# A 31-tap depthwise convolution on TensorE in 16 passes of two taps instead of 31 of one, with its passes and VectorE's taps at other places in the attention, and the first weight slab used chunk by chunk

## The chip, the cores and the metric

The kernel runs on one core of a Trainium2 chip. The metric is the device time in microseconds (us) of one execution. The engines are TensorE (PE in the profile; its weight loads are PEld), VectorE (DVE), ScalarE (ACT), GpSimd (POOL) and SyncE (SP, which issues most DMAs). Each takes its own instructions in order and waits for others by semaphores.

## The reference

Two transformer blocks over 512 positions of width 1024 run one after the other, all in float32. The first has a 3-tap convolution branch, a stick-breaking attention and an MLP; the second a parallel mixer, a cross attention over 256 memory rows and a gated MLP. The mixer of the second block is where most of the change lies:

```
z = h @ w_in                                  # h: 512 x 1024, RMS-normed
a = z[:, :512] * sigmoid(z[:, 512:1024])      # 512 channels
a[t, c] = sum_k conv_dw[k, c] * a[t + k - 15, c] + b[c]     # k = 0 .. 30
a = silu(layernorm(a))                        # over the 512 channels
q, k = rope(rmsnorm(q)), rope(rmsnorm(k))     # 8 query heads, 2 key/value heads of 64
att = softmax(q @ k.T / 8) @ v                # no mask, 512 x 512 scores per head
y = concat(a, att) @ w_out
```

The other part of the change lies at the first product of the first block, `h @ w_in`, with h the normed and modulated input.

## The kernel before

**Products.** A float32 product is made of three fp32r matmuls (`mm3`, L811 to L814): high by high, high by low and low by high parts. POOL splits each 1 MB weight slab of 128 x 2048 into `w_hi` (L687, for slab 0 L695) and `w_lo` (L689, for slab 0 L700), in the order in which PE uses them; three slabs are in flight. ACT and DVE split the activations into `ht_hi` and `ht_lo`, eight chunks of 128 x 512.

**First slab.** Slab 0 holds four chunks of 128 rows (k = 0 to 3) of four output groups (m = 0 to 3) of `h @ w_in`. POOL makes its low part in four pieces, one for each m, and counts them in `first_lo`. In `features` (called with `first=True`), PE takes group 0 with its four chunks, each as soon as its chunk of h is split, then groups 1, 2 and 3. So each group has its own bank of PSUM (PE's output memory, eight banks) and is finished with slab 1.

**The 31-tap convolution.** Channels lie on the partitions in four chunks, positions along the row, padded by 15 on both sides (`av`). POOL does chunk 3. DVE does chunks 0 and 1, 62 taps, each one scalar-tensor-tensor instruction of 128 x 512 (L1857) that adds into bank 7. PE does chunk 2: a pass of plain float32 for each tap, with a diagonal 128 x 128 matrix as weights (`tap_of`, made by ACT from the identity in L1651) and the shifted 512 columns of `av` as moving data, all into bank 6 (L1234). A plain float32 matmul leaves two MATMUL records in the trace.

**Attention of the second block.** Four pairs of heads; a pair has four score tiles (n = 0 to 15 over all pairs), one for each 128 queries, and each tile has two halves, one for each head (32 halves in all). `ATT2_ORDER` (L225 to L235) sets the order for every engine:

- `zz` n: PE makes the scores of tile n, two matmuls of 64 rows (L1195). For each half DVE takes the maximum (TENSOR_REDUCE, L2223), scales it (L1864) and, one half later, inverts the sum of the half before (RECIPROCAL, L1868). ACT does the exponential (L1697). The probabilities are scaled by ACT for pairs 0 and 1 and by POOL for pairs 2 and 3.
- `conv` n: PE does `PE_TAPS[n]` taps (3, 3, 3, 3 with pair 0; 3, 3, 2, 2 with pair 1; 2, 1, 1, 1 with pair 2; 2, 1, 1 with pair 3). After the last, ACT adds the bias and stores the chunk.
- `tt` n: PE transposes the probabilities of the pair before (L1209), ACT copies them out (L1715). `oo` p: PE multiplies pair p with the values, four key chunks by two heads of 64 columns (L1221). ACT and DVE split the result.
- `l` 0: PE sums the convolution's output over the channels (L1248). It waits until all four chunks are complete. `l` 1 sums the squares.

The scores of pair p + 1 stand between the transposes of pair p, and `oo` p - 1 stands behind the first score tile of pair p + 1. Of DVE's 62 taps, 20 stand between the rotary steps and 16 behind the keys. The other 26 are spread by `fill(per_tile)`, where `per_tile` works out to 1: one tap behind each half, which is used up with half 26. What is left of them is done before DVE's part of `l` 0 (`for _ in taps`).

Of the kernel before, what the change touches and what calls it, by code (L numbers as in the profile page):

```python
# [19 lines left out]
ALU = mybir.AluOpType  # L20
# [5 lines left out]
P = 128  # L26
# [240 lines left out]
def build(nc, A, out):  # L267
    with ExitStack() as ctx:
# [126 lines left out]
        with ExitStack() as lend:  # L395
# [270 lines left out]
        def _(g):  # L666
# [128 lines left out]
        def _(pe):  # L795
# [27 lines left out]
            def features(t0, ks, ah, al, i=None, tper=0, sper=0, n=T, each=None, first=False, behind=None):  # L823


                for s in range(ks):
# [546 lines left out]
        def _(act):  # L1373
# [243 lines left out]
            act.wait_ge(tables_loaded, 16 * 6)  # L1617
            st.done(act.activation(rope_gq[:], rope[:, 0], ACT.Copy, scale=qkg[:, 0:1]), tables_made)
# [105 lines left out]
            for what, n in ATT2_ORDER:  # L1724
# [120 lines left out]
        def _(v):  # L1845
# [603 lines left out]
```

## Time and profile before

| | |
|---|---|
| runs | 1513.2, 1512.0, 1512.74 us, median 1512.74 |
| the profiled execution | 1516.2 us, its span 1514.5 us |
| PE busy | 1463.9 us, 97% of the span |
| POOL, DVE, ACT busy | 917.3, 736.0, 452.0 us |
| PE's share of the chain that ended last | 85% (DVE 8%, ACT 3%, DMA 2%) |
| the second block's attention, from its first scores to `l` 0 | 879.8 to 949.0 us |

The span is one profiled execution; its own time lies 1.7 us above its span and 3.5 us above the median of the three timed runs. PE is busy nearly everywhere. So a stretch in which PE waits for another engine, or in which the chain of waits runs over another engine, is an exception and is to be read by itself: there the share over the whole span says nothing.

### The profile page before, as it was taken

Reading aid. Unit: us, or ns where it says so; the run is one execution under the profiler, and the core shown is the slowest. Engines: PE = TensorE matmul, PEld = TensorE weight load, DVE = VectorE, ACT = ScalarE, POOL = GpSimd, SP = SyncE. Lnnn points to the kernel's source line nnn. Section 1 sums busy time; section 2 is a strip of 40 time slices with the busy share of each in tenths; the row PEclk is TensorE's granted clock in tenths of the full one; section 3 lists DMA queues with packets and bytes.
Section 4 is the critical chain, followed back from the end, with each engine's and each line's share of the span. In section 5 each row is a group of like instructions: output and inputs, shape, how many; then the busy total and the mean of one; then the engine's idle time right before and its main releaser. Section 6 shows DMA issues by size and latency. Waiting matters only on the chain.

```text
span 1514.5 us, 18342 instructions
## 1 busy us (share of the span) xinstructions
PE 1463.9 (97%) x7071; PEld 1187.7 (78%) x7071; DVE 736.0 (49%) x1121; ACT 452.0 (30%) x924; POOL 917.3 (61%) x361
## 2 busy tenths in 40 slices
PE   3999999999999999999999999999999999999997
PEld 3788777768898888888898854689779888888886
DVE  6898146544541211212262877532416555455656
ACT  3201133323520110201142466533324433333213
POOL 1857454345656565656566997266234889788651
PEclk9999999999999999999999999999999999999999
DMA  9765221223322323232243200123023423232131
GB/s 332 299 252 219 98 84 56 84 84 99 125 98 84 111 84 112 84 111 84 84 147 112 84 29 1 56 94 130 28 84 112 139 84 112 84 111 84 56 102 65
DMA packets 94099, 162.59 MB, mean 107 GB/s; under 512 B 3597, under 2 KB 44481, under 8 KB 94017
## 3 DMA queue, kind: packets, MB, share of 16 engines
q1 hardware_dynamic: 90896, 155.20, 30.1%
q10 hardware_dynamic: 3121, 6.26, 1.2%
q8 instruction: 56, 0.92, 0.2%
q14 instruction: 26, 0.21, 0.0%
HBM read 159.35 MB, written 2.10 MB: 107 GB/s over the span
## 4 chain that ended last, share of the span: by engine, by line
PE 85%; DVE 8%; ACT 3%; DMA 2%; issue 1%; POOL 0%; DVEq 0%; SPq 0%; ACTq 0%; POOLq 0%
PE bank L812 26%; PE bank L813 26%; PE bank L814 26%; DVE bank L1857 2%; DMA ada_w<-in_w_ada 1%; DVE smx L2223 1%; PE bank L1221 1%; DVE x L1853 1%; DVE bank L1853 1%; PE bank L1291 1%; PE bank L1272 1%; PE bank L1065 1%; PE bank L1088 1%; ACT junk L1402 1%; PE bank L1248 0%
## 5 line engine op out<-in xcount | busy, mean ns | idle before, releaser
L689 POOL TENSOR_TENSOR w_lo<-w_raw,w_hi 128x2048 fp32r<-128x2048 f32 x111 | 516.8, 4656 | 9.3
L687 POOL TENSOR_SCALAR w_hi<-w_raw 128x2048 fp32r<-128x2048 f32 x111 | 216.0, 1946 | 480.4 <-DMA w_raw<-in_w_in 116.5
L812 PE MATMUL bank<-ht_hi,w_hi 128*128 128x512 f32 (+1 forms) x1200 | 444.1, 370 | 0.8 <-DVE ht_lo L1853 0.8
L813 PE MATMUL bank<-ht_hi,w_lo 128*128 128x512 f32 (+1 forms) x1200 | 441.0, 368 | 0.0
L814 PE MATMUL bank<-ht_lo,w_hi 128*128 128x512 f32 (+1 forms) x1200 | 440.8, 367 | 0.0
L812 PEld LDWEIGHTS bank<-ht_hi,w_hi 128*128 128x128 f32 x1200 | 227.1, 189 | 42.7 <-DVE ht_lo L1853 2.6
L814 PEld LDWEIGHTS bank<-ht_lo,w_hi 128*128 128x128 f32 x1200 | 227.0, 189 | 37.2
L813 PEld LDWEIGHTS bank<-ht_hi,w_lo 128*128 128x128 f32 x1200 | 227.2, 189 | 36.8 <-issue 0.5
L1857 DVE SCALAR_TENSOR_TENSOR uc<-bank,par,uc 128x511 f32<-128x511 f32 x88 | 66.0, 750 | 128.1 <-ACT uc L1801 125.4
L1853 DVE TENSOR_TENSOR facc<-bank,facc 128x512 f32<-128x512 f32 x64 | 44.3, 692 | 114.9 <-PE bank L814 111.2
L814 PE MATMUL bank<-w_lo,hq_hi 128*128 128x512 f32 x256 | 99.6, 389 | 0.0
L812 PE MATMUL bank<-w_hi,hq_hi 128*128 128x512 f32 x256 | 99.6, 389 | 0.0
L813 PE MATMUL bank<-w_hi,hq_lo 128*128 128x512 f32 x256 | 99.6, 389 | 0.0
L1594 ACT ACTIVATE hr<-bank 128x512 f32<-128x512 f32 x32 | 19.2, 599 | 261.8 <-PE bank L814 261.0
L812 PE MATMUL bank<-w_hi,ht_hi 128*128 128x512 f32 x224 | 88.2, 394 | 0.0
L1801 ACT ACTIVATE uc<-bank,par 128x512 f32<-128x512 f32 x44 | 34.4, 781 | 177.3 <-PE bank L814 177.1
L814 PE MATMUL bank<-w_lo,ht_hi 128*128 128x512 f32 x224 | 87.2, 389 | 0.0
L813 PE MATMUL bank<-w_hi,ht_lo 128*128 128x512 f32 x224 | 87.2, 389 | 0.0
L1857 DVE SCALAR_TENSOR_TENSOR ada_acc<-ada_w,cvec,ada_acc 128x1024 f32<-128x1024 f32 x42 | 80.3, 1911 | 11.5 <-DMA ada_w<-in_w_ada 8.2
L1853 DVE TENSOR_TENSOR bank<-bank,hr 128x512 f32<-128x512 f32 x32 | 22.4, 700 | 122.4 <-ACT hr L1594 122.3
L757 POOL TENSOR_TENSOR dn_lo<-dn_raw,dn_hi_all 128x1024 fp32r<-128x1024 f32 x28 | 67.0, 2406 | 18.0 <-ACT dn_hi_all L1780 17.9
L1853 DVE TENSOR_TENSOR ht_lo<-bank,ht_hi 128x512 fp32r<-128x512 f32 x60 | 41.5, 692 | 32.3 <-ACT ht_hi L1540 20.3
(294 smaller groups left out, 2216.0 us busy)
## 6 DMA issues: line engine op xcount, KB each, us to landing
w_raw<-in_w_in SPq DMA_DIRECT2D x27, 1024.0 KB, 5.0
ada_w<-in_w_ada SPq DMA_DIRECT2D x48, 512.0 KB, 7.2
w_raw<-in_w_up SPq DMA_DIRECT2D x22, 1024.0 KB, 4.9
w_raw<-in_w_mlp_in SPq DMA_DIRECT2D x16, 1024.0 KB, 5.4
w_raw<-in_w_mlp_out SPq DMA_DIRECT2D x16, 1024.0 KB, 5.0
w_raw<-in_w_out SPq DMA_DIRECT2D x8, 1024.0 KB, 5.0
w_raw<-in_w_mem_kv SPq DMA_DIRECT2D x8, 1024.0 KB, 5.1
dn_raw<-in_w_down SPq DMA_DIRECT2D x16, 512.0 KB, 4.8
```

The costliest lines, as they stand in the source:

```text
L687: g.tensor_scalar(w_hi[:, r], w_raw[:, r], 1.0, 1.0, ALU.mult, ALU.mult).then_inc(slab_hi, 1)
L689: g.tensor_tensor(w_lo[:, r], w_raw[:, r], w_hi[:, r].bitcast(F32), ALU.subtract).then_inc(slab_split, 1)
L757: g.tensor_tensor(dn_lo[:, w], dn_raw[:, w], dn_hi(w).bitcast(F32), ALU.subtract).then_inc(dn_split, 1)
L812: inc_free(pe.matmul(o, ah, bh, start=start, stop=False))
L813: pe.matmul(o, al, bh, start=False, stop=False)
L814: return pe.matmul(o, ah, bl, start=False, stop=stop)
L1065: pe.matmul(t.ap[:, 0:W1[qt]], q1[o, p, qt * P:qt * P + P], k1[o, p, 0:W1[qt]], start=True, stop=True).then_inc(t.full, 1)
L1088: ins = pe.matmul(t.ap[HD * j:HD * j + HD, kc * P:T], v1[:, kc, h * HD:h * HD + HD], at1[:, j, A1[kc]:A1[kc + 1]], start=kc == 0, stop=kc ...
L1594: st.done(act.activation(hr[:, m % 2], t.ap[:], ACT.Relu), hr_ready)
L1801: st.done(act.activation(uc[:, c], tiles[c].ap[:], ACT.Identity, scale=par[:, p, 2 + g, k:k + 1], bias=par[:, p, 6 + g, k:k + 1]), uc_ready)
L1853: do(v.tensor_tensor(o, a, b, op), sem, tile)
L1857: do(v.scalar_tensor_tensor(out=o, in0=a, scalar=s, in1=b, op0=op0, op1=op1), sem, tile)
```

## The change

**First slab.** POOL makes the low part in four pieces by chunk k (all four groups) instead of by group m. PE takes a chunk's products for the groups begun so far as soon as this chunk is there: first (0, 0), then (0, 1), (1, 0), (1, 1), and so on, as (m, k).

**Convolution on PE.** `av2` holds chunk 2 twice: partitions 0 to 63 have the channels of one half g, partitions 64 to 127 the same channels shifted by one position. Four DMAs on ACT's queue copy it. The weights are 128 x 64: two diagonals, one for tap 2k and one for tap 2k + 1. One pass for g = 0 writes partitions 0 to 63 of bank 6, one for g = 1 partitions 64 to 127. So there are 16 pairs of passes, 32 matmuls of 64 output rows. ACT makes 32 weight matrices of 128 x 64 instead of 31 of 128 x 128, and some small operands for them (`ident2`, `tap_w`, two DMAs to `cdw_x`).

**Places.** PE's pairs stand behind the tiles 0 to 8, as 3, 3, 3, 2 with pair 0, 1, 1, 1, 1 with pair 1 and 1 with tile 8. DVE's 26 late taps: none with pair 0, one behind each half of pairs 1, 2 and 3 (24), and the last two before `l` 0.

```diff
-PE_TAPS = (3, 3, 3, 3, 3, 3, 2, 2, 2, 1, 1, 1, 2, 1, 1)
+TAP_PAIRS = (K2 + 1) // 2
+PE_TAP_PAIRS = (3, 3, 3, 2, 1, 1, 1, 1, 1)
...
-                for m in range(4):
-                    c = slice(m * P, m * P + P)
-                    g.tensor_tensor(lo[:, :, c], raw[:, :, c], hi[:, :, c].bitcast(F32), ALU.subtract).then_inc(
-                        first_lo if m < 3 else slab_split, 1)
+                for k in range(4):
+                    g.tensor_tensor(lo[:, k], raw[:, k], hi[:, k].bitcast(F32), ALU.subtract).then_inc(
+                        first_lo if k < 3 else slab_split, 1)
...
+                    if by_pieces:
+                        for new in range(4):
+                            each(new)
+                            Tile(t0 + new).wait_free(pe)
+                            pe.wait_ge(first_lo if new < 3 else slab_split, new + 1 if new < 3 else 1)
+                            for m, k in [(m, new) for m in range(new)] + [(new, k) for k in range(new + 1)]:
+                                c = slice(m * P, m * P + P)
+                                mm3(Tile(t0 + m).ap[:, 0:n], wh[:, k, c], wl[:, k, c], ah[:, k], al[:, k], k == 0, False)
...
-                    pe.wait_ge(taps_made, K2)
-                    Tile(T0["w_in2a"] + 4 + DVE_CC).wait_taken(pe)
-                k0 = sum(PE_TAPS[:i])
-                for k in range(k0, k0 + PE_TAPS[i]):
-                    ins = pe.matmul(t.ap[:], tap_of(k), av[:, DVE_CC, k:k + T], start=k == 0, stop=k == K2 - 1)
-                if k == K2 - 1:
+                    pe.wait_ge(taps_made, 2 * TAP_PAIRS)
+                    pe.wait_ge(av2_loaded, 16 * 4)
+                k0 = sum(PE_TAP_PAIRS[:i])
+                for k in range(k0, k0 + PE_TAP_PAIRS[i]):
+                    for g in range(2):
+                        ins = pe.matmul(t.ap[HC * g:HC * g + HC, :], tap_m[:, k, g], av2[:, g, 2 * k:2 * k + T], start=k == 0,
+                                        stop=k == TAP_PAIRS - 1)
+                if k == TAP_PAIRS - 1:
...
-            for k in range(K2):
-                w = V_CDW + CC * k + DVE_CC
-                st.done(act.activation(tap_of(k), ident[:], ACT.Copy, scale=vec[:, w:w + 1]), taps_made)
+            Tile(T0["w_in2a"] + 4 + DVE_CC).wait_taken(act)
+            avc = av[:].rearrange("p c t -> p (c t)")
+            for half in range(2):
+                for g in range(2):
+                    at = DVE_CC * (T + 2 * pad) + half
+                    act.dma_start(av2[HC * half:HC * half + HC, g, :],
+                                  avc[HC * g:HC * g + HC, at:at + T + 2 * pad]).then_inc(av2_loaded, 16)
...
+            for k in range(TAP_PAIRS):
+                for g in range(2):
+                    st.done(act.activation(tap_m[:, k, g], ident2[:], ACT.Copy, scale=tap_w[:, k, g:g + 1]), taps_made)
...
-            per_tile = -(-(DVE_CC * K2 - sum(TAPS_BEFORE_ROPE) - TAPS_BEHIND_K) // (H1 * NT))
...
-                        fill(per_tile)
+                        fill(n >= NT)
```

Line numbers of the changed file differ: L812 is L811, L1195 is L1202, L1234 is L1242, L1209 is L1216, L1857 is L1886, L2223 is L2251.

On PE, at the second and third group of three matmuls of slab 0 (bank 2 is group m = 0, bank 3 is group 1), before:

```order
L812 MATMUL bank2<-ht_hi,w_hi 128x512
L813 MATMUL bank2<-ht_hi,w_lo 128x512
L814 MATMUL bank2<-ht_lo,w_hi 128x512
L812 MATMUL bank2<-ht_hi,w_hi 128x512
L813 MATMUL bank2<-ht_hi,w_lo 128x512
L814 MATMUL bank2<-ht_lo,w_hi 128x512
```

and now:

```order
L811 MATMUL bank2<-ht_hi,w_hi 128x512
L812 MATMUL bank2<-ht_hi,w_lo 128x512
L813 MATMUL bank2<-ht_lo,w_hi 128x512
L811 MATMUL bank3<-ht_hi,w_hi 128x512
L812 MATMUL bank3<-ht_hi,w_lo 128x512
L813 MATMUL bank3<-ht_lo,w_hi 128x512
```

The second group is the same, (0, 1); the third was (0, 2), which needs chunk 2 of h, and is (1, 0), which needs chunk 0.

On PE, at the first score tiles of pair 0 (bank 6 is the convolution's, `x3` counts like instructions in a row), before:

```order
L1195 MATMUL bank4<-k2,q2 128x512
L1195 MATMUL bank5<-k2,q2 128x512
L1234 MATMUL bank6<-av,tap_low 128x512 x3
L1195 MATMUL bank0<-k2,q2 128x512
L1195 MATMUL bank1<-k2,q2 128x512
L1234 MATMUL bank6<-av,tap_low 128x512
L1234 MATMUL bank6<-av,not_before 128x512
L1234 MATMUL bank6<-av,tap_m 128x512
```

and now:

```order
L1202 MATMUL bank4<-k2,q2 128x512
L1202 MATMUL bank5<-k2,q2 128x512
L1242 MATMUL bank6<-av2,tap_m 64x512 x6
L1202 MATMUL bank0<-k2,q2 128x512
L1202 MATMUL bank1<-k2,q2 128x512
L1242 MATMUL bank6<-av2,tap_m 64x512 x6
```

Three taps of 128 output rows behind a tile became six matmuls of 64 output rows, which do six taps.

On DVE, at the last three halves of pair 3 and DVE's part of `l` 0 (`ay<-bank2,ay`), before:

```order
L2223 TENSOR_REDUCE smx<-bank1 128x1
L1864 TENSOR_SCALAR smx<-smx,qks 128x1
L1868 RECIPROCAL smx<-smx 128x1
L2223 TENSOR_REDUCE smx<-bank4 128x1
L1864 TENSOR_SCALAR smx<-smx,qks 128x1
L1868 RECIPROCAL smx<-smx 128x1
L2223 TENSOR_REDUCE smx<-bank5 128x1
L1864 TENSOR_SCALAR smx<-smx,qks 128x1
L1868 RECIPROCAL smx<-smx 128x1 x2
L1857 SCALAR_TENSOR_TENSOR ay<-bank2,ay 128x512 x4
```

and now:

```order
L2251 TENSOR_REDUCE smx<-bank4 128x1
L1893 TENSOR_SCALAR smx<-smx,qks 128x1
L1897 RECIPROCAL smx<-smx 128x1
L1886 SCALAR_TENSOR_TENSOR bank7<-av,vec,bank7 128x512
L2251 TENSOR_REDUCE smx<-bank5 128x1
L1893 TENSOR_SCALAR smx<-smx,qks 128x1
L1897 RECIPROCAL smx<-smx 128x1
L1886 SCALAR_TENSOR_TENSOR bank7<-av,vec,bank7 128x512
L1897 RECIPROCAL smx<-smx 128x1
L1886 SCALAR_TENSOR_TENSOR bank7<-av,vec,bank7 128x512
L1886 SCALAR_TENSOR_TENSOR ay<-av,vec,bank7 128x512
L1886 SCALAR_TENSOR_TENSOR ay<-bank2,ay 128x512 x4
```

Behind each half stands a tap (`bank7<-av,vec,bank7`), and two more stand between the last reciprocal and `l` 0; before, no tap stood here.

## Rows read from the trace of the kernel before

**Rows 1.** which lines hold the chain of waits, 880 to 970 us, by share

```profile
by line: DVE smx L2223 18.7%; DVE bank L1857 17.0%; PE bank L1221 16.2%; PE bank L1248 8.1%; ACT pt L1715 7.1%; DVE smx L1864 6.0%; issue 5.6%; PE bank L1195 4.7%; DVE smx L1868 3.9%; PE bank L1209 3.2%; ACT p2d L1697 1.9%; PE bank L1234 1.
```

**Rows 2.** busy time in one stretch: us, PE, PEld, DVE, ACT, POOL, PEclk, DMA

```profile
931.70:949.00 17.30, 15.79 (x72) 7.35 (x72) 12.60 (x31) 11.51 (x26) 5.77 (x9) 1.00 0.01 1
```

**Rows 3.** timeline of PE, 879 to 950 us: start, us, engine, line, tiles, idle before

```profile
879.82 1.13 PE L1195 MATMUL bank<-k,q 64*128 64x512 f32 x4
...
880.88 2.84 PE L1234 MATMUL bank<-av,tap_low 128*128 128x512 f32 x6
...
883.65 1.13 PE L1195 MATMUL bank<-k,q 64*128 64x512 f32 x4
...
916.77 3.65 PE L1221 MATMUL bank<-pt,v 128*64 128x512 f32 x16 [1.40 <-ACT pt L1715]
...
922.43 1.12 PE L1234 MATMUL bank<-av,tap_m 128*128 128x512 f32 x2
...
949.04 3.70 PE L1248 MATMUL bank<-ay,ones 128*128 128x512 f32 x8 [0.31 <-ACT pt L1715]
```

**Rows 4.** timeline of DVE, 868 to 952 us

```profile
868.35 1.55 DVE L1857 SCALAR_TENSOR_TENSOR bank<-av,vec,bank 128x512 f32<-128x512 f32 x2
...
880.98 0.69 DVE L2223 TENSOR_REDUCE smx<-bank 128x1 f32<-128x512 f32 x1 [3.39 <-PE bank L1195]
...
898.15 0.69 DVE L2223 TENSOR_REDUCE smx<-bank 128x1 f32<-128x512 f32 x1
...
914.97 0.69 DVE L2223 TENSOR_REDUCE smx<-bank 128x1 f32<-128x512 f32 x1
...
921.08 0.69 DVE L1853 TENSOR_TENSOR ht_lo<-bank,ht_hi 128x512 fp32r<-128x512 f32 x1 [2.28 <-ACT ht_hi L1540]
...
922.53 0.69 DVE L2223 TENSOR_REDUCE smx<-bank 128x1 f32<-128x512 f32 x1 [0.76 <-PE bank L1195]
...
935.40 0.69 DVE L2223 TENSOR_REDUCE smx<-bank 128x1 f32<-128x512 f32 x1
...
941.76 0.69 DVE L2223 TENSOR_REDUCE smx<-bank 128x1 f32<-128x512 f32 x1 [0.77 <-PE bank L1195]
...
947.74 0.69 DVE L2223 TENSOR_REDUCE smx<-bank 128x1 f32<-128x512 f32 x1 [0.41 <-PE bank L1195]
...
951.04 0.17 DVE L1868 RECIPROCAL smx<-smx 128x1 f32<-128x1 f32 x1 [0.60 <-ACT p2d L1697]
```

**Rows 5.** timeline of ACT at the diagonal matrices, 838 to 852 us

```profile
839.54 7.72 ACT L1651 ACTIVATE tap_m<-ident,vec 128x128 f32<-128x128 f32 x26
...
851.88 0.59 ACT L1496 COPY k<-bank 128x512 f32<-128x512 f32 x1 [4.62 <-PE bank L1153]
```

**Rows 6.** timeline of ACT's queue near 44 us, one DMA issue

```profile
44.13 0.35 ACTq L1392 DMA_DIRECT2D ada_b<-in_b_ada  x1
```

**Rows 7.** timeline of PE in the first slab, 42 to 47 us

```profile
42.42 0.79 PE L812 MATMUL bank<-ht_hi,w_hi 128*128 128x512 f32 x1 [0.49 <-DVE ht_lo L1853]
...
45.14 0.63 PE L812 MATMUL bank<-ht_hi,w_hi 128*128 128x512 f32 x1
45.57 0.63 PE L813 MATMUL bank<-ht_hi,w_lo 128*128 128x512 f32 x1
...
46.54 0.40 PE L813 MATMUL bank<-ht_hi,w_lo 128*128 128x512 f32 x1
46.77 0.40 PE L814 MATMUL bank<-ht_lo,w_hi 128*128 128x512 f32 x1
```

**Rows 8.** timeline of POOL in the first slab

```profile
36.69 4.97 POOL L700 TENSOR_TENSOR w_lo<-w_raw,w_hi 128x512 fp32r<-128x512 f32 x4
```

**Rows 9.** line L1221 on PE's weight port: count, ns min/median/max

```profile
L1221 PEld LDWEIGHTS bank<-pt,v x64: 132/137/137, 916.7 to 963.8; 128*64 128x64 f32 x64
```

**Rows 10.** busy time in two stretches near 230 us, columns as in group 2

```profile
228.00:232.00 4.00, 1.34 (x8) 0.89 (x7) 3.83 (x4) 1.09 (x2) 1.98 (x1) 1.00 0.00 0
232.00:236.00 4.00, 3.34 (x22) 3.04 (x24) 1.90 (x3) 2.34 (x8) 0.00 (x0) 0.74 0.00 0
```

More of the change, by code:

```diff
@@ L41 @@
 DVE_CC = CC - POOL_CC - PE_CC
-PE_TAPS = (3, 3, 3, 3, 3, 3, 2, 2, 2, 1, 1, 1, 2, 1, 1)
+TAP_PAIRS = (K2 + 1) // 2
+PE_TAP_PAIRS = (3, 3, 3, 2, 1, 1, 1, 1, 1)
 POOL_PAIRS = 2
-LOW_TAPS = 4
 ADA_BUFS = 7
@@ L229 @@
             ATT2_ORDER += [("zz", NT * (_p + 1) + _m)]
-            ATT2_ORDER += [("conv", NT * (_p + 1) + _m)] * (NT * (_p + 1) + _m < len(PE_TAPS))
+            ATT2_ORDER += [("conv", NT * (_p + 1) + _m)] * (NT * (_p + 1) + _m < len(PE_TAP_PAIRS))
         ATT2_ORDER += [("oo", _p - 1)] * (_m == 0 and _p >= 1)
@@ L325, in build @@
         with ExitStack() as lend:
-            tap_low = sb("tap_low", [P, LOW_TAPS, P], where=lend)
-        with ExitStack() as lend:
             s2 = sb("s2", [P, 2, 2 * P], where=lend)
@@ L406, in build @@
         pt2 = sb("pt2", [P, 2, NT, T], where=ph)
-        tap_m = sb("tap_m", [P, K2 - LOW_TAPS - 1, P], where=ph)
+        HC = P // 2
+        tap_m = sb("tap_m", [P, TAP_PAIRS, 2, HC], where=ph)
+        av2 = sb("av2", [P, 2, T + 2 * pad], where=ph)
+        tap_w = sb("tap_w", [P, TAP_PAIRS, 2], where=ph)
+        cdw_x = sb("cdw_x", [P, K2 * CC], where=ph)
+        ident2 = sb("ident2", [P, HC], where=ph)
         ph.close()
@@ L447, in build @@
             "gated", "y_gated", "o_hi", "a1_sig", "a1_scanned", "sm_max", "sm_inv", "sm_p"))
-        taps_made = sem("taps_made")
+        taps_made, av2_loaded = sem("taps_made"), sem("av2_loaded")
         tables_made, q_squared, rope_std, ln_std = (sem(n) for n in (
@@ L518, in sums_made @@
             return sum(0 if not by_sums(r) else 2 if r % 2 == 0 else 4 for r in range(j))
-        def tap_of(k):
-            return tap_low[:, k] if k < LOW_TAPS else not_before[:] if k == LOW_TAPS else tap_m[:, k - LOW_TAPS - 1]
         block = ctx.enter_context(nc.Block())
@@ L834, in features @@
                     wh, wl = wv(r, 4)
+                    if by_pieces:
[6 more added lines that the diff above has]
+                                mm3(Tile(t0 + m).ap[:, 0:n], wh[:, k, c], wl[:, k, c], ah[:, k], al[:, k], k == 0, False)
+                        state["owed"] += 1
+                        continue
                     for m in range(4):
@@ L838, in features @@
                             t.wait_free(pe)
-                        if by_pieces:
-                            pe.wait_ge(first_lo if m < 3 else slab_split, m + 1 if m < 3 else 1)
                         for k in range(4):
@@ L1609, in _ @@
                                   A[name].rearrange("(p o) -> p o", o=1)).then_inc(tables_loaded, 16)
+            for g in range(2):
+                act.dma_start(cdw_x[HC * g:HC * g + HC, :],
+                              vec[HC - HC * g:P - HC * g, V_CDW:V_CDW + K2 * CC]).then_inc(tables_loaded, 16)
             t0 = T0["w_in2a"]
@@ L1616, in _ @@
                 st.done(act.activation(t.ap[:], t.ap[:], ACT.Sigmoid), gated)
-            act.wait_ge(tables_loaded, 16 * 6)
+            act.wait_ge(tables_loaded, 16 * 8)
             st.done(act.activation(rope_gq[:], rope[:, 0], ACT.Copy, scale=qkg[:, 0:1]), tables_made)
@@ L1648, in _ @@
             st.done(act.activation(t.ap[:], t.ap[:], ACT.Sqrt, bias=eps_t[:, 0:1], scale=1.0 / HD), rope_std)
-            for k in range(K2):
-                w = V_CDW + CC * k + DVE_CC
-                st.done(act.activation(tap_of(k), ident[:], ACT.Copy, scale=vec[:, w:w + 1]), taps_made)
+            Tile(T0["w_in2a"] + 4 + DVE_CC).wait_taken(act)
[5 more added lines that the diff above has]
+                                  avc[HC * g:HC * g + HC, at:at + T + 2 * pad]).then_inc(av2_loaded, 16)
+            own = vec[:, V_CDW:V_CDW + K2 * CC].rearrange("p (k c) -> p k c", c=CC)
+            other = cdw_x[:].rearrange("p (k c) -> p k c", c=CC)
+            st.done(act.activation(tap_w[:, TAP_PAIRS - 1, :], ident[:, 0:2], ACT.Copy, scale=0.0))
+            st.after()
+            for half in range(2):
+                h = slice(HC * half, HC * half + HC)
+                st.done(act.copy(ident2[h, :], ident[h, h]))
+                for g in range(2):
+                    st.done(act.copy(tap_w[h, 0:TAP_PAIRS - half, g], (own if g == half else other)[h, half::2, DVE_CC]))
+            st.after()
+            for k in range(TAP_PAIRS):
+                for g in range(2):
+                    st.done(act.activation(tap_m[:, k, g], ident2[:], ACT.Copy, scale=tap_w[:, k, g:g + 1]), taps_made)
             for g in range(KV2):
@@ L1735, in _ @@
                 elif what == "conv":
-                    if n == len(PE_TAPS) - 1:
+                    if n == len(PE_TAP_PAIRS) - 1:
                         t = Tile(T0["conv31_pe"])
```

## The prediction

> **What bounds the kernel now.** I read the busy table first: PE is busy for 97% of the span, so most edits that take PE work away would pay in full. The exception is the place where this change works. The chain of waits through the second block's attention, 880 to 970 us, has DVE's maxima (L2223) with 18.7% and DVE's taps (L1857) with 17.0% ahead of any line of PE; PE's convolution (L1234) is the last one named, with under 2% [rows 1]. So DVE sets the pace here, though PE looks busy beside it. The timeline of DVE says where. From the first half of pair 1 at 898.15 to the first half of pair 2 at 914.97 eight halves pass in 16.82 us, 2.10 us each, with no wait [rows 4]: maximum, scale, reciprocal and one tap. In pair 3, where the taps have run out, the four halves from 941.76 to 947.74 take 5.98 us, 1.50 us each, and the wait printed there is one for PE's scores (0.41) [rows 4]: from there on PE sets the pace, with 15.79 us busy of 17.30 against DVE's 12.60 [rows 2]. So pairs 0 to 2 are DVE's, pair 3 is PE's, and `l` 0 follows at once on PE at 949.04, 0.31 us late [rows 3].
>
> **The change part by part.** I call DVE's unit a half (32 of them) and PE's unit a tile (16).
>
> *PE's passes.* Three taps behind tile 0 take 883.65 - 880.88 = 2.77 us, the score pair 880.88 - 879.82 = 1.06, together 3.83 a tile. Two records, one tap, show 1.12 us and six show 2.84, so a tap more costs 0.86 [rows 3]. Nothing in the program before has the new form exactly, but L1221 has its shape: 128 rows by 64 columns, alternately into the lower and upper half of one bank, plain float32. Its 16 records, 8 matmuls, take 3.65 us [rows 3], 0.91 for two of them, where 0.86 each would be 6.9. So the two halves run side by side, and a pair of passes costs one tap of before. Blocks of 3 pairs stay at 2.77, the block of 2 is 2.77 - 0.86 = 1.9. Fifteen taps' worth of PE time, 15 x 0.86 = 13 us, are gone, mostly behind tiles 4 to 14.
>
> *Pair 0.* Tile 3's scores start at 879.82 + 3 x 3.83 = 891.3. DVE follows 1.16 us behind (880.98 against 879.82), 892.5, and with no tap between its last two halves it needs from the first maximum of a tile to the end of the pair's last reciprocal what it needed in pair 3: 951.04 + 0.17 - 947.74 = 3.47 us [rows 4]. Pair 1 starts on DVE at 896.0 instead of 898.15: gain 2.1 us. The end of tile 4's scores, 891.3 + 1.06 + 1.9 + 1.06 = 895.3, is not later. The eight taps taken out of pair 0 gain no more than that, since PE's three-pair blocks fill the room.
>
> *Pairs 1 and 2.* A tap stands behind each half before and after; DVE keeps 2.10 us a half, and PE's shorter blocks only make PE wait. The stalls at `oo` 0 (2.28 and 0.76 us [rows 4]) hang on ACT's copies behind DVE's last reciprocal of the pair, so they move with DVE. Nothing gained, nothing lost: pair 3 starts at 935.40 - 2.1 = 933.3.
>
> *Pair 3.* Its first two halves had taps already, so half 27 starts at 941.76 - 2.1 = 939.66. Then six halves now carry a tap: 6 x 2.10 = 12.6, to 952.3. The last reciprocal adds 0.2, and the two taps left over 1.55 + 0.1 (868.35 shows two in a row in 1.55 [rows 4]): 954.2. PE may not start `l` 0 until the last of them is done. So `l` 0 starts at 954.2 instead of 949.04, **5.2 us later**. Behind `l` 0 stands everything: the value product of pair 2, the transposes of pair 3, the layer norm and w_out. PE waits for no transfer there that could take this back. Bounds: 4.5 if DVE comes out of pair 0 another 0.7 earlier (the reciprocal hidden), 6.0 if the new blocks cost 0.3 more per tile for switching shapes.
>
> *First slab.* PE waited 0.49 us at 42.42 for chunk 2 of h [rows 7]; now it has (1, 0) and (1, 1) to do meanwhile. In the stretch it runs at 45.57 - 45.14 = 0.43 us a matmul and later at 46.77 - 46.54 = 0.23 [rows 7], 1.2 and then 2.4 GHz. If the faster clock comes at the same moment, 0.49 us of slow work is worth 0.49 x 0.23 / 0.43 = 0.26 us; if it comes earlier by the whole wait, 0.5; if it comes 2 us earlier since PE works without a break, another 2 x (1 - 0.23 / 0.43) = 0.9, 1.4 in all. I take 0.5, the wait itself, nearest to the row. POOL's pieces are the same size, 4.97 / 4 = 1.24 us each, the last at 41.7 [rows 8], before PE needs it.
>
> *ACT's new work.* 32 weight matrices at 7.72 / 26 = 0.30 us each against 31, seven small copies at no more than 0.30, four DMA issues at 0.35 [rows 6] and about 0.3 of waiting: 0.3 + 2.1 + 1.4 + 0.3 = 4.1 us. ACT sat idle for 4.62 us before its next work at 851.88 [rows 5]. I cost it at nothing; if that cover is short by 0.5 us, the keys' copies are late by as much, and PE has its w_in slabs to do. At the other end it is nothing too. The copies to `av2` have from about 840 to 880.9 to land. Storing PE's chunk moves from tile 14 to tile 8 and stands where ACT waits for `oo` 0 anyway.
>
> Sum: -2.1 (pair 0) + 7.3 (pair 3 and the two leftover taps: 954.2 + 2.1 - 949.04) - 0.5 (slab 0) = **+4.7 us**. For the profiled execution 1516.2 + 4.7 = 1520.9; it lay 3.5 above the median of the runs, so the median becomes 1512.74 + 4.7 = 1517.4.
>
> One rule speaks against the side-by-side passes. In L1221 the 64 weight loads last 0.137 us each [rows 9], and all of them fit beside the matmuls within those 3.65 us a product. The Trainium skill (TensorE: Matmul & The Clock Gate, Part 3, What overlaps and what doesn't) says that a weight load overlaps running matmuls only where it goes to another row group. Both column halves use all rows; by that rule 12 loads of a three-pair block would stand open, 12 x 0.137 = 1.6 us a tile. Row and rule differ here; I follow the row and keep the rule as a small rival.
>
> **The rivals.**
>
> *A, forecast:* as above, 1517.4, its own range 1515.8 to 1519.2.
>
> *B, the clock falls in pair 3.* PE's work there is 1.9 of 4.2 us a tile: 5.98 / 2 = 2.99 before, less a one-tap block of 2.77 - 2 x 0.86 = 1.05. For it: near 230 us PE was busy 1.34 of 4 us and the next 4 us were granted 0.74 [rows 10]. Against: with waits of 1.4 us the stage kept 1.00, as [rows 2] shows for pair 3. At half speed the pair itself stays hidden behind DVE, but `l` 0 (3.6 us) could take twice as long: 1517.4 + 3.6 = 1521.0.
>
> *C, the stalls between pairs close.* If shorter PE blocks let `oo` 0 and `oo` 1 come earlier, DVE's 2.28 + 0.76 and 0.77 us [rows 4] go: -3.8, that is 1513.6, no measurable change. Against: those waits end with ACT's copies, behind DVE's own last reciprocal.
>
> *D, faster: PE sets the pace in pair 3 also after the change.* Price: l 0 comes 2.1 us earlier from pair 0, and two one-tap blocks of 1.05 us (tiles 13 and 14) are gone, -4.2, with slab 0 -4.7: 1508.0. It needs the tap to fit into DVE's wait for scores. It decides at 1.50 us a half in pair 3: below that with a tap, the kernel is faster; at 2.10, A holds. Only 0.41 us a tile of waiting is there for two taps.
>
> *E, the change does not do what it says: the passes of a pair run one after the other.* A block of 3 pairs is 6 x 0.86 = 5.2, a tile 6.3, the block of two 3.5; tile 4's scores end at 879.82 + 3 x 6.3 + 1.06 + 3.5 + 1.06 = 904.3, pair 1 starts 6.2 late instead of 2.1 early: 1517.4 + 8.3 = 1525.7. Against it: L1221.
>
> *F, the open weight loads* of the rule above: a tile 3.83 + 1.6, pair 1 starts about 3.2 late: 1517.4 + 5.3 = 1522.7.
>
> **How the numbers follow.** Chances: A 0.66, B 0.10, C 0.08, D 0.06, E 0.05, F 0.05. About 0.2%, 3.0 us, is what a measurement here can tell from no change: 1509.7 to 1515.8. Faster: D and a sliver of C, 0.07. The same: the rest of C and A's low end, 0.14. Slower: 0.79. The range starts below C, at 1513.0, leaving out D, and ends above B, at 1521.5, leaving out E and most of F: about 0.16 left out.
>
> **What would show it.** Right: DVE's maxima in pair 3 at 2.10 us spacing where they had 1.50; `l` 0 about 74 us behind the first scores (69.2 before), with PE waiting for a DVE tap ahead of it; PE's blocks of six 64-row matmuls as long as three taps were; pair 1's first maximum 16.2 us behind the first scores (18.3 before); the gap at slab 0 gone, and PE's pitch from 0.43 to 0.23 at about the same moment. Wrong: a pitch under 2.10 with taps, six matmuls in 5 us, PE waiting in pair 0 for `av2` or the weights, or a stage behind `l` 0 that is shorter than before.

## The result: 12 us slower, more than twice the forecast

| | before | after |
|---|---|---|
| median of 8 runs each, us | 1513.45 (1511.64 to 1515.04) | 1525.55 (1518.33 to 1526.34) |
| ratio, 95% interval | | 1.0077 [1.0063, 1.0092] |
| profiled execution, its span | 1516.2, 1514.5 | 1523.3, 1521.5 |
| PE busy | 1463.9 | 1453.3 |
| first matmul of slab 0 to first scores | 841.2 | 836.5 |
| first scores to `l` 0 | 69.2 | 77.8 |
| `l` 0 to w_out | 18.8 | 21.3 |
| w_out to the end of the span | 546.6 | 548.1 |

The forecast was 1517.4 with a range up to 1521.5. The sign was right, the size was not: the medians are 12.1 us apart, the ratio makes 1513.45 x 0.0077 = 11.7 us, and 4.7 was forecast. PE is busy for 10.6 us less, and the kernel is slower. The last four rows of the table cut one profile of each kernel into four parts. The attention stage, from the first scores to w_out, grew by 8.55 + 2.49 = 11.0 us, and the part behind it by 1.5. The first part differs by 4.6 us in the other direction, but that is no gain: in the twelve profiles of this study it took 836.3 to 841.2 us, also where the code ahead of it was the same; 836.3 came with the old order of slab 0. In before, the granted clock stood low for a while near 180 us, and again near 236 [rows 10]. Two rows of its windows table (columns as in [rows 2]):

```profile
176.00:180.00 4.00, 4.00 (x28) 3.28 (x28) 1.89 (x5) 0.00 (x0) 0.00 (x0) 0.91 0.28 116
180.00:184.00 4.00, 4.00 (x11) 2.51 (x10) 2.77 (x4) 0.00 (x0) 0.00 (x0) 0.66 0.16 37
```

PE is busy for the whole of both rows, and the second has 0.66 of the clock. Right ahead of the fall PE did 32 matmuls of one column (175.22 to 178.7). In eleven of the twelve profiles the clock is low for a while behind these matmuls, between 175 and 183 us, for a shorter or a longer time; in three, before among them, it is low between 228 and 238. Before also came to its full pitch in slab 0 5.6 us later than after did. By the pitches of [rows 7] that costs before 2.6 us, and its two windows from 232 to 240 us, with a clock of 0.74 and 0.84, cost it up to 1.7 more. This estimate, 4.3, is nearly the whole of the 4.6 us. So I compare stages and not spans.

**DVE did as forecast.** The timeline of DVE after the change, to be laid beside [rows 4]; the maxima are L2251 now, the taps L1886, the reciprocals L1897:

```profile
875.46 0.69 DVE L2251 TENSOR_REDUCE smx<-bank 128x1 f32<-128x512 f32 x1 [3.34 <-PE bank L1202]
...
890.33 0.69 DVE L2251 TENSOR_REDUCE smx<-bank 128x1 f32<-128x512 f32 x1
...
914.95 0.69 DVE L1882 TENSOR_TENSOR ht_lo<-bank,ht_hi 128x512 fp32r<-128x512 f32 x1 [3.98 <-ACT ht_hi L1549]
...
935.83 0.69 DVE L1882 TENSOR_TENSOR ht_lo<-bank,ht_hi 128x512 fp32r<-128x512 f32 x1 [2.70 <-ACT ht_hi L1549]
937.29 0.69 DVE L2251 TENSOR_REDUCE smx<-bank 128x1 f32<-128x512 f32 x1 [0.77 <-PE bank L1202]
...
947.96 0.69 DVE L2251 TENSOR_REDUCE smx<-bank 128x1 f32<-128x512 f32 x1
...
950.32 0.76 DVE L1886 SCALAR_TENSOR_TENSOR bank<-av,vec,bank 128x512 f32<-128x512 f32 x1
951.11 0.75 DVE L1886 SCALAR_TENSOR_TENSOR ay<-av,vec,bank 128x512 f32<-128x512 f32 x1
```

Pair 1's first maximum stands 16.0 us behind the first scores (874.30), where 16.2 was forecast. In pair 3 five steps from 937.29 to 947.96 take 10.67 us, 2.13 each, forecast 2.10, and the two left-over taps end at 951.86. What was not forecast are the waits at the splits of the value products: 3.98 us where [rows 4] has 2.28, and 2.70 for pair 1, where before had 0.69:

```profile
940.30 0.69 DVE L1853 TENSOR_TENSOR ht_lo<-bank,ht_hi 128x512 fp32r<-128x512 f32 x1 [0.69 <-ACT ht_hi L1540]
```

**PE shows why.** Its timeline, to be laid beside [rows 3]; two-tap passes are L1242, value products L1228, `l` 0 is L1257:

```profile
874.30 1.13 PE L1202 MATMUL bank<-k,q 64*128 64x512 f32 x4
875.36 2.79 PE L1242 MATMUL bank<-av,tap_m 128*64 128x512 f32 x12
878.09 1.13 PE L1202 MATMUL bank<-k,q 64*128 64x512 f32 x4
...
908.94 5.35 PE L1228 MATMUL bank<-pt,v 128*64 128x512 f32 x16 [2.67 <-ACT pt L1744]
...
925.66 1.37 PE L1202 MATMUL bank<-k,q 64*128 64x512 f32 x4 [0.40 <-ACT pt L1744]
...
929.86 5.32 PE L1228 MATMUL bank<-pt,v 128*64 128x512 f32 x16 [2.83 <-ACT pt L1744]
...
952.07 6.19 PE L1257 MATMUL bank<-ay,ones 128*128 128x512 f32 x8 [5.82 <-DVE ay L1886]
```

For pair 1's product before had this row:

```profile
935.99 3.65 PE L1221 MATMUL bank<-pt,v 128*64 128x512 f32 x16 [1.16 <-ACT pt L1715]
```

The 12 records of three pairs of passes take 2.79 us, as three single taps did. But the value products of pairs 0 and 1 take 5.3 us where the same 16 records took 3.65, and `l` 0 takes 6.19 instead of 3.70. Each of the three comes right behind a wait of PE. The windows table of after says what happened (granted clock behind POOL's column):

```profile
904.00:908.00 4.00, 2.14 (x8) 0.53 (x8) 3.48 (x8) 3.62 (x8) 3.63 (x5) 1.00 0.00 0
908.00:912.00 4.00, 3.06 (x9) 1.16 (x11) 2.66 (x6) 3.02 (x7) 3.82 (x4) 0.67 0.00 0
...
924.00:928.00 4.00, 2.02 (x8) 0.75 (x8) 3.48 (x8) 2.50 (x7) 3.73 (x6) 0.80 0.00 0
928.00:932.00 4.00, 2.14 (x6) 0.85 (x8) 3.55 (x8) 2.59 (x6) 1.38 (x2) 0.50 0.00 0
...
948.00:952.00 4.00, 0.00 (x0) 0.00 (x0) 3.45 (x7) 1.83 (x4) 1.38 (x2) 0.50 0.00 0
952.00:956.00 4.00, 3.93 (x5) 1.85 (x6) 0.00 (x0) 0.00 (x0) 0.00 (x0) 0.50 0.00 0
```

The same stretch of before had 1.00 in every window, with PE busy for 4.00 us of the four in 904:908 and 3.83 in 924:928:

```profile
904.00:908.00 4.00, 4.00 (x20) 2.07 (x19) 3.45 (x9) 3.62 (x9) 3.64 (x5) 1.00 0.00 2
...
924.00:928.00 4.00, 3.83 (x20) 2.06 (x20) 3.45 (x9) 2.50 (x7) 3.97 (x1) 1.00 0.00 0
```

PE has lost work that nobody waited for. It stands idle more, the clock falls to 1.2 GHz, and the next product, for which DVE does wait, runs at that clock. The wait right ahead isn't the whole of it. For pair 1 the clock fell before that wait: the scores at 925.66 already take 1.37 us where others take 1.13, and the waits of PE ahead of them were of 1.43 us at most. The chain of waits over the stretch of [rows 1] has the value products on top now:

```profile
by line: PE bank L1228 19.9%; DVE smx L2251 16.4%; DVE bank L1886 16.2%; PE bank L1257 6.9%; ACT pt L1744 6.5%; PE bank L1242 5.4%; DVE smx L1893 5.3%; issue 4.9%; PE bank L1202 4.7%; DVE smx L1897 3.7%; PE bank L1216 2.3%; ACT p2b L1726 1.
```

L1228 rose from 16.2% to 19.9%. But these 90 us begin 5.7 us later in after's stage than in before's. Taken from the first scores to w_out of each kernel, the value products' line rose from 16.5% to 18.1% and the line of `l` 0 and `l` 1 from 7.8% to 9.5%, which is 3.4 and 2.5 us; the maxima fell from 19.1% to 14.9% and the taps from 17.4% to 14.7%. So my theory of the 11.0 us: 5.2 as forecast (DVE's late taps less what pair 0 gains), 1.7 + 1.7 from the value products of pairs 0 and 1, 2.5 from `l` 0, together 11.1.

### The profile page after: what moved, and what is told of

Same layout as the page of the kernel before. It is cut to its first block, busy times and chain, and to the rows that moved or that the text cites. A ratio compares the mean times of both kernels' runs of the same rounds, so it can differ in the third digit from the quotient of the medians.

```text
span 1521.5 us, 18360 instructions
## 1 busy us (share of the span) xinstructions
PE 1453.3 (96%) x7073; PEld 1179.7 (78%) x7073; DVE 740.9 (49%) x1121; ACT 451.8 (30%) x932; POOL 919.1 (60%) x361
## 4 chain that ended last, share of the span: by engine, by line
PE 84%; DVE 8%; ACT 3%; DMA 2%; POOL 1%; issue 1%; DVEq 0%; SPq 0%; ACTq 0%; POOLq 0%
PE bank L811 25%; PE bank L813 25%; PE bank L812 25%; DVE bank L1886 2%; PE bank L1228 1%; DMA ada_w<-in_w_ada 1%; DVE smx L2251 1%; DVE x L1882 1%; DVE bank L1882 1%; PE bank L1300 1%; PE bank L1281 1%; PE bank L1257 1%; PE bank L1072 1%; PE bank L1095 1%; POOL w_lo L689 1%
## 5 line engine op out<-in xcount | busy, mean ns | idle before, releaser
L811 PE MATMUL bank<-ht_hi,w_hi 128*128 128x512 f32 (+1 forms) x1200 | 442.7, 369 | 0.5 <-DVE ht_lo L1882 0.5
L812 PE MATMUL bank<-ht_hi,w_lo 128*128 128x512 f32 (+1 forms) x1200 | 440.0, 367 | 0.0
L811 PEld LDWEIGHTS bank<-ht_hi,w_hi 128*128 128x128 f32 x1200 | 226.4, 189 | 41.1 <-issue 2.1
L812 PEld LDWEIGHTS bank<-ht_hi,w_lo 128*128 128x128 f32 x1200 | 226.5, 189 | 36.7 <-issue 0.5
L1886 DVE SCALAR_TENSOR_TENSOR uc<-bank,par,uc 128x511 f32<-128x511 f32 x88 | 66.0, 750 | 128.3 <-ACT uc L1830 125.6
L811 PE MATMUL bank<-w_hi,hq_hi 128*128 128x512 f32 x256 | 99.6, 389 | 0.0
L812 PE MATMUL bank<-w_hi,hq_lo 128*128 128x512 f32 x256 | 99.6, 389 | 0.0
L1886 DVE SCALAR_TENSOR_TENSOR ada_acc<-ada_w,cvec,ada_acc 128x1024 f32<-128x1024 f32 x42 | 85.0, 2023 | 7.3 <-DMA ada_w<-in_w_ada 3.5
L811 PE MATMUL bank<-w_hi,ht_hi 128*128 128x512 f32 x224 | 88.2, 394 | 0.0
L812 PE MATMUL bank<-w_hi,ht_lo 128*128 128x512 f32 x224 | 87.2, 389 | 0.0
```

Source lines behind the costliest of these rows:

```text
L811: inc_free(pe.matmul(o, ah, bh, start=start, stop=False))
L812: pe.matmul(o, al, bh, start=False, stop=False)
L1886: do(v.scalar_tensor_tensor(out=o, in0=a, scalar=s, in1=b, op0=op0, op1=op1), sem, tile)
```

## The experiments

Kernels that were timed in one go share the runs of the kernel before: the first four here (1512.55 us), the next four (1514.21) and the last two (1513.42). "Stage" is from the first scores to w_out, from one profile each (88.1 before, 99.1 changed).

| edit | median us (range) | ratio to before, 95% | first scores to `l` 0 | stage | value products 0, 1 | `l` 0 |
|---|---|---|---|---|---|---|
| slab edit alone | 1511.10 (1507.3 to 1513.4) | 0.999 [0.998, 1.000] | 69.2 | 88.1 | 3.65, 3.65 | 3.70 |
| late DVE taps alone | 1522.04 (1520.7 to 1525.3) | 1.0061 [1.0046, 1.0077] | 76.1 | 96.8 | 3.65, 3.65 | 5.49 |
| changed, DVE taps even | 1515.18 (1509.7 to 1518.4) | 1.0009 [0.9995, 1.0024] | 69.8 | 88.7 | 3.65, 5.12 | 3.68 |
| changed, PE busy, not ahead of the products | 1522.56 (1517.7 to 1524.4) | 1.0060 [1.0042, 1.0078] | 79.6 | 98.4 | 5.35, 5.35 | 3.67 |
| changed, DVE taps from tile 2 | 1518.44 (1515.3 to 1521.2) | 1.0033 [1.0018, 1.0047] | 73.4 | 92.6 | 5.35, 5.32 | 3.68 |
| taps even and passes even | 1515.17 (1510.2 to 1518.2) | 1.0010 [0.9999, 1.0022] | 72.2 | 91.1 | 3.65, 5.35 | 3.68 |
| changed, slab as before | 1523.99 (1519.3 to 1526.8) | 1.0067 [1.0046, 1.0087] | 77.9 | 99.2 | 5.35, 5.40 | 6.25 |
| changed kernel again | 1525.13 (1517.9 to 1526.3) | 1.0062 [1.0040, 1.0083] | 77.8 | 99.3 | 5.35, 5.35 | 6.34 |
| changed, PE busy ahead of the products | 1517.76 (1511.0 to 1519.1) | 1.0022 [1.0007, 1.0037] | 75.0 | 93.7 | 3.65, 3.65 | 3.60 |
| taps even, PE busy ahead of the products | 1512.50 (1509.5 to 1517.7) | 0.9999 [0.9987, 1.0010] | 68.5 | 87.3 | 3.65, 3.65 | 3.68 |

### The slab edit alone

The kernel before with the two edits of the first slab (POOL's pieces by k, PE's order by chunks), which the diff above shows, and nothing else.

> The kernel before with only the first slab's edit. Theory 1 (the edit is worth its wait and perhaps an earlier rise of the clock): the 0.5 us gap inside slab 0 is gone, time 0.5 to 4 us below before, nothing else moves, and the attention of the second block takes the same 69.2 us from its first scores to l 0. Theory 2 (the 12 us of the changed kernel partly come from here, by another phase of PE against its clock in the whole program): slower by 1 us or more.

1511.10 against 1512.55 us, -1.4, at the edge of what the interval can tell. PE's timeline at slab 0, for [rows 7]:

```profile
38.79 0.63 PE L813 MATMUL bank<-ht_lo,w_hi 128*128 128x512 f32 x1
39.52 0.49 PE L811 MATMUL bank<-ht_hi,w_hi 128*128 128x512 f32 x1
39.85 0.39 PE L812 MATMUL bank<-ht_hi,w_lo 128*128 128x512 f32 x1
40.08 0.40 PE L813 MATMUL bank<-ht_lo,w_hi 128*128 128x512 f32 x1
```

The pitch of 0.23 us is there at 39.85, 2.05 us behind slab 0's first matmul (37.80), where before it came after 7.65. That is 5.6 us earlier; the prediction's bound of -1.4 was for 2 us earlier. The edit doesn't fix the moment, though: with it the pitch fell after 1.7 to 4.4 us in nine profiles, and after 4.1 us in both other profiles with the old order. So the 7.65 us of [rows 7] belong to that profile more than to the order, and how much the edit gains is not settled to a microsecond.

### DVE's late taps alone

```diff
-                        fill(per_tile)
+                        fill(n >= NT)
```

This is the kernel before, with PE's one-tap passes, and DVE's late taps moved as the change moves them.

> The kernel before (31 one-tap passes on PE, first slab as before) with only DVE's late taps moved: none with pair 0, one behind each half of pairs 1 to 3. Theory 1 (DVE's taps in pair 3 make DVE the bound and PE idle ahead of l 0): l 0 about 7 us later than before (76 us behind the first scores), PE waits several us ahead of it, and l 0 itself runs at the lower clock, 6.2 instead of 3.7 us: 9 to 10 us slower than before; the value products of pairs 0 and 1 stay at 3.65 us, since PE has its long passes there. Theory 2 (the two-tap passes are what costs): at most 2 us slower than before.

+9.5 us, most of the loss with one line. PE's rows:

```profile
914.09 3.65 PE L1221 MATMUL bank<-pt,v 128*64 128x512 f32 x16 [0.90 <-ACT pt L1715]
...
933.32 3.65 PE L1221 MATMUL bank<-pt,v 128*64 128x512 f32 x16 [1.16 <-ACT pt L1715]
...
953.86 5.49 PE L1248 MATMUL bank<-ay,ones 128*128 128x512 f32 x8 [5.82 <-DVE ay L1857]
```

`l` 0 comes 6.9 us later (69.2 to 76.1) and is 1.8 us longer. The wait ahead of it is the same 5.82 us as in the changed kernel. Both value products stay at 3.65: with the long one-tap passes PE was busy enough and waited only 0.90 and 1.16 us for ACT. So the late taps are enough for a slow `l` 0, and the slow value products need the work taken from PE.

The late taps by themselves put `l` 0 off by 6.9 us, and not by the 5.2 of the theory. The two-tap passes give 1.7 of it back. With one-tap passes pair 1's first maximum comes 16.5 us behind the first scores and pair 2's another 18.1 us later, with waits of DVE for scores of 0.87 and 0.61 us in between; in the changed kernel it is 16.0 and 16.8.

### The changed kernel with DVE's taps as before

```diff
-                        fill(n >= NT)
+                        fill(1)
```

> The changed kernel with DVE's late taps as before, one behind each half from pair 0 on until they run out. Theory 1 (late taps cost 5 to 6 us and the low clock in l 0; PE's shorter blocks cost the low clock in the value products of pairs 0 and 1): l 0 about 68 us behind the first scores plus 1.7 for each value product at 5.3 us, l 0 itself 3.7 us: 0 to 3 us slower than before, 9 or more below the changed kernel. Theory 2 (the clock falls only because of the late taps): value products at 3.65 us, 1 to 2 us faster than before. Theory 3 (the passes themselves): still 8 us or more slower than before.

The difference to before falls from 12.1 to 2.6 us, which can't be told from none, and `l` 0 is at 69.8 us and 3.68 long. What is left in the stage is one slow value product (5.12 against 3.65) less a gain of 0.9 us. The two-tap passes, with 13 us less work for PE, bring nothing here that the time shows.

### PE kept busy at the transposes of pairs 1 and 2 and ahead of `l` 0

```diff
+                if what == "zz" and h == 10:
+                    Tile(T0["conv31_pe"]).wait_taken(pe)
+                if what == "l" and h == 0:
+                    keep_busy(5)
+                if what == "tt" and 6 <= h < 12:
+                    keep_busy(2)
```

`keep_busy` issues plain float32 matmuls of 128 x 512 into the idle bank 6; their results aren't used.

> The changed kernel with idle time of PE in pairs 2 and 3 filled: two more plain float32 matmuls of 128 x 512 ahead of each transpose step 6 to 11 and five ahead of l 0, into the convolution's bank after its result is taken; their results are not used. Theory 1 (the low clock follows from PE's idle time): value product of pair 1 back to 3.65 and l 0 to 3.7 us, that of pair 0 still 5.3; time 4 us below the changed kernel although PE does 17 matmuls more. Theory 2 (the low clock has another cause, or the stage is bound by DVE alone): no change, or slower by what the matmuls push aside.

`l` 0 is back at 3.67, at one place behind which only the idle time had changed: the clock is shown to be the cause there. The value products stayed at 5.35, pair 1's too, against the expectation. None of the useless work stood right ahead of them, where PE still waited 2.68 and 3.08 us for ACT. And a piece of it behind pair 1's product held up tile 13's scores by 1.8 us, so the stage gained only 0.7.

### DVE's taps from tile 2

```diff
-                        fill(n >= NT)
+                        fill(n >= NT // 2)
```

> The changed kernel with DVE's late taps from score tile 2 on instead of tile 4 (26 halves from the fifth of pair 0), so that none is left over at l 0 and the last two halves of pair 3 have none. Theory 1 (each tap in pair 3 or at l 0 adds what it takes, pair 0 holds some for nothing): l 0 about 73 us behind the first scores (77.8 in the changed kernel, 69.8 with taps from tile 0), PE waits 1 to 2 us ahead of it, l 0 at 3.7 us; 5 to 7 us below the changed kernel. Theory 2 (the passes' places decide, not the taps'): no change to the changed kernel.

`l` 0 follows the dose: 69.8, 73.4 and 77.8 us behind the first scores for taps from tile 0, 2 and 4 on. Of the first step, 3.5 us, 1.7 are pair 0's value product, which is slow here and was not with taps from tile 0.

### Taps even and passes even

```diff
-PE_TAP_PAIRS = (3, 3, 3, 2, 1, 1, 1, 1, 1)
+PE_TAP_PAIRS = (1, 1, 1, 1, 2, 2, 2, 2, 1, 1, 1, 1)
...
-                        fill(n >= NT)
+                        fill(1)
```

> The changed kernel with DVE's late taps from tile 0 on and PE's pairs of passes spread as 1, 1, 1, 1 with pair 0, 2, 2, 2, 2 with pair 1, 1, 1, 1, 1 with pair 2. Theory 1 (the value products of pairs 0 and 1 run at the lower clock since PE has short blocks ahead of them): both at 3.65 us, the stage from the first scores to w_out 87 us (88.1 before), the kernel 1 to 3 us faster than the kernel before. Theory 2 (the low clock is there whatever PE does with two-tap passes): a value product at 5.1 us or more again, the kernel 1 us or more slower than before.

Two pairs of passes behind each tile of pair 1 leave PE with a shorter wait before pair 0's product (1.60 us) and that product at 3.65. Pair 1's still runs at 5.35, behind a wait of 3.65, so the expectation of two fast products failed. The median is the same as with the passes in front (1515.2), though `l` 0 is 2.4 us later in the profile. The two profiles are not of like executions: this one took 1517.89 us, near the top of its twelve runs, and the other 1515.15, which is its median to 0.03. In this one PE waits 6.90 us at the start of pair 1 and then runs its transposes and scores at the low clock, the scores in 2.08 us instead of 1.13. Whether it does so in every execution isn't shown.

### The changed kernel with the first slab as before, and the changed kernel again

The first slab's two edits taken back; beside it the changed kernel itself.

> The changed kernel with the first slab as before. Theory 1 (the slab's edit gains 1 to 2 us by itself and the attention's change costs 11 to 13): 1 to 2 us slower than the changed kernel. Theory 2 (the slab's edit is worth nothing, or harms in this company): the same or faster.

> The changed kernel itself beside these three. Theory 1: 11 to 13 us slower than before, its stage from the first scores to w_out 97 to 101 us, with the low clock in l 0 and in one or both value products; where the low clock falls differs from run to run and explains the spread of 8 us between its runs. Theory 2 (the second profile shows the full clock everywhere in this stage): then the stage is 94 us and the rest is elsewhere.

1523.99 and 1525.13, six runs each: the slab's edit can't be told from nothing in this company. The stage is 99.2 and 99.3 us, as in the first profile (99.1), so the loss is all there without the slab. The low clock fell on the same three products each time. So it does not explain the whole spread between the runs: the two profiled executions of the changed kernel are 3.05 us apart (1523.27 and 1526.32) and their stages 0.2, while the part ahead of the stage differs by 2.6 (836.5 and 839.1).

### PE kept busy right ahead of the three slow products

The theory said 5.9 of the 11.0 us are clock, and only 2.5 of them had been shown. Here the useless matmuls stand where PE waits, and write into the bank that the next product starts anew:

```diff
                 t = Tile(TT2["oo", p])
                 t.wait_free(pe)
+                for _ in range(3 if p < 2 else 0):
+                    pe.matmul(t.ap[:], ident[:], av2[:, 0, 0:T], start=True, stop=True)
...
                 t = Tile(TT2["l", what])
                 t.wait_free(pe)
+                for _ in range(0 if what else 5):
+                    pe.matmul(t.ap[:], ident[:], av2[:, 0, 0:T], start=True, stop=True)
```

> The changed kernel with three matmuls of no use (plain float32, 128 x 512, each two records, 0.86 us at full clock) right ahead of the value products of pairs 0 and 1, where PE waited 2.67 and 2.83 us for ACT, and five right ahead of l 0, where it waited 5.8 us for DVE. They write into the bank that the product behind them then starts anew; their results aren't used. Theory (of the 11.0 us by which the attention stage grew, 1.7 + 1.7 + 2.5 are these three products at half clock because PE has stood still before them): the value products of pairs 0 and 1 back at 3.65 us, l 0 at 3.7, l 0 about 74.3 us behind the first scores, the stage 99.1 - 5.9 = 93.2 us, the time 1525.1 - 5.9 = 1519.2. Rival 1 (the value products are slow because of the short one-tap blocks and the transposes before them, over the whole of pairs 1 and 2, not because of the wait just ahead): they stay at 5.3 us, only l 0 recovers, stage 96.6 us, time 1522.6. Rival 2 (the useless work gets in the way): the value products are 3.65 but start 1 to 2 us later, the stage stays at 96 us or more.

PE's timeline:

```profile
906.74 2.84 PE L1224 MATMUL bank<-av,ident 128*128 128x512 f32 x6
909.51 3.65 PE L1230 MATMUL bank<-pt,v 128*64 128x512 f32 x16
...
925.59 2.84 PE L1224 MATMUL bank<-av,ident 128*128 128x512 f32 x6
928.73 3.65 PE L1230 MATMUL bank<-pt,v 128*64 128x512 f32 x16 [0.30 <-ACT pt L1748]
...
943.70 6.30 PE L1253 MATMUL bank<-av,ident 128*128 128x512 f32 x10
949.83 3.60 PE L1261 MATMUL bank<-ay,ones 128*128 128x512 f32 x8
```

All three products are back, and with them 5.4 us of the stage (99.1 to 93.7) and some 7 us of the time: 4.3 us above before's median, where the changed kernel was 12.1 and 10.9 above. The part behind w_out is shorter too, 546.8 us against 548.1 and 547.9. Both rivals fall; pair 0's product starts 34.7 us behind the first scores, as it did in the changed kernel (34.6). The third block of useless work stands across the return of the clock: its five matmuls take 1.26 us each on average where those ahead of the value products take 0.95, since the clock is low when they start, and behind them `l` 0 runs at full speed. Windows of the same profile:

```profile
936.00:940.00 4.00, 2.22 (x14) 1.17 (x12) 3.42 (x8) 2.44 (x7) 1.21 (x2) 1.00 0.00 0
940.00:944.00 4.00, 2.98 (x13) 1.93 (x10) 3.49 (x7) 2.44 (x7) 1.39 (x2) 0.57 0.00 0
944.00:948.00 4.00, 4.00 (x6) 1.57 (x6) 3.40 (x8) 2.70 (x6) 1.81 (x3) 0.58 0.00 0
948.00:952.00 4.00, 4.00 (x11) 1.73 (x10) 1.02 (x2) 0.00 (x0) 0.27 (x1) 1.00 0.00 0
```

With the clock repaired, what is left is the forecast: `l` 0 at 75.0 us behind the first scores where 74 was forecast, the stage 5.7 us longer than before where 5.2 was, the time +1.1 to +5.6 us by the interval where 4.7 was.

### The same with DVE's taps as before

The three useless matmuls ahead of the value products of pairs 0 and 1, and `fill(1)`.

> The changed kernel with DVE's taps one behind each half from the start, as before the change, and with three matmuls of no use ahead of the value products of pairs 0 and 1 (their results aren't used). Theory (what is left there against before is one value product at half clock, 5.12 against 3.65 us, with two-tap passes that otherwise cost nothing): both value products 3.65 us, l 0 68.3 us behind the first scores, time 1515.2 - 1.5 = 1513.7, no different from the kernel with the slab's edit alone (1511) by more than 3 us. Rival (the product of pair 1 stays slow): 1515.2, l 0 at 69.8.

1512.50 us. The value products are both at 3.65, and the stage (87.3) is even 0.8 us shorter than before's; the time can't be told from before's or from that of the slab edit alone. 1511.10 us for the slab edit alone stays the best median, and it needs none of the rest.

## Why the prediction was too small

**What held.** *PE's passes*: 2.79 us for three pairs, forecast 2.77, and the 64 weight loads of 136 ns each were hidden in all the passes, so the rule that rival F rests on did not hold here. Rivals E and F are refuted: each would have put pair 1 later, and it came earlier. *Pair 0*: a gain of 2.3 us (18.3 to 16.0), forecast 2.1. *Pair 3*: halves with a tap at 2.13 us, forecast 2.10, and PE waiting for the last tap; rival D, which wanted less than 1.50, is refuted. *ACT's new work*: 7.76 us for 32 matrices, and no wait of PE for it or for `av2`. *First slab*: -1.4 alone, with an interval from -3.0 to 0, where -0.5 was taken; the two bounds of the prediction go by how much earlier the clock rises, and that varied more between profiles than by the order; in company not to be told from zero.

**The step that failed** is the one on pairs 1 and 2: "PE's shorter blocks only make PE wait. [...] Nothing gained, nothing lost". The wait was forecast, and what it does to the next product was not. The value product behind it is one of the few places in these pairs where DVE waits for PE, and it became 1.7 us longer, twice. DVE's split waited 3.98 us where [rows 4] has 2.28, the same 1.7 more; for pair 1 it was 2.70 against 0.69. I had looked for the end of rival C there, that the stalls would close, and argued that ACT's copies hold them; I did not ask whether they could grow.

**The size that failed** is `l` 0's. Its wait was forecast, and rival B had the low clock behind it as a loss of up to 3.6 us, at a chance of 0.10. It was 2.5 and 2.6 us in the two profiles of the changed kernel and 1.8 in the one with late taps alone. B had put the low clock in pair 3 only, and not at the value products. [rows 2] was the wrong witness: it shows 1.00 with PE busy for 15.8 of 17.3 us, and the change took that busy time away. The same microseconds of after's span, which lie 5.5 us later in its stage, hold 11.28:

```profile
931.70:949.00 17.30, 11.28 (x58) 5.21 (x54) 11.97 (x27) 8.87 (x20) 4.15 (x6) 0.89 0.01 1
```

[rows 10], busy 1.34 of 4 us and then a clock of 0.74, was the row nearest to what came, and it had been put against one place only. Summed up: 5.2 forecast, + 1.7 + 1.7 + 2.5 = 11.1, measured 11.0 in the stage. That the two terms are clock is shown by the useless work ahead of these products, which took 5.4 us of them back.

**What is left.** The part behind w_out is 1.1 to 1.5 us longer than before's 546.6 in seven of the nine profiles with two-tap passes, both of the changed kernel among them. In all seven PE waits once for POOL's low part of an MLP slab, as this row of PE's waits in after says (total, times, longest):

```profile
PE bank L811 <- POOL dn_lo L756: 1.5, 1, 1.5
```

It is absent from the three profiles with one-tap passes and from one of the two with useless work ahead of `l` 0, and 0.2 us in the other; in these five this part is 546.5 to 546.8 us. Why POOL is late there is open. Open too is why pair 0's product stayed fast in the kernel with even taps (3.65 us behind a wait of 2.67) and pair 1's did not (5.12 behind 2.46): the wait right ahead doesn't decide alone. In the second case the clock was low before the wait began, as the scores ahead of it show, which take 1.13 us at full clock:

```profile
928.99 1.75 PE L1202 MATMUL bank<-k,q 64*128 64x512 f32 x4 [0.40 <-ACT pt L1744]
```

## What to carry to other kernels

Work that PE does in a wait is not free to take away: ask for each gap that the change opens what PE does next, whether another engine waits for that, and what it costs at the lower clock (here 1.7 us for 8 plain float32 matmuls of 64 output rows, 2.5 us for 4 of 128). A row that shows the clock staying up counts only for as much idle time as that row had. And where another engine sets the pace, moving its work towards the end of a stage costs the whole of what no longer fits, whatever PE saves.

## What the hardware showed that I had not expected

- A value product took 3.65 us behind waits of 0.90 to 1.60 us and 5.1 to 5.4 behind waits of 2.46 to 3.65 us, but behind 2.67 us it also took 3.65 once.
- The clock came back while PE went on working: in the kernel with PE busy ahead of the products it was granted 0.58 in the window from 944 us and 1.00 in the one from 948, within a block of five matmuls, and the four behind it took 0.90 us each.
- The clock was low also where PE's records leave no gap: 0.66 from 180 us in before, behind 32 matmuls of one column.
- Single runs of one kernel spread by more than 8 us (1509.69 to 1518.35 in one set of 12, 1507.46 to 1517.03 in 21 of before); the stage in the profiles repeated to 0.2 us (99.1, 99.3, 99.2).
